# The ring of weight slots moved by 192 bytes in every partition

## What is computed

```python
def swiglu(x, w_gate, w_up, w_down):
    return (jax.nn.silu(x @ w_gate) * (x @ w_up)) @ w_down
...
x = layer_norm(ALPHA * x + 0.5 * swiglu(x, ffn_w_gate[l, 0], ffn_w_up[l, 0], ffn_w_down[l, 0]), ln_g[l, 0], ln_b[l, 0])
x = layer_norm(ALPHA * x + hybrid_mixer(x, w_in[l], ...), ln_g[l, 1], ln_b[l, 1])
x = layer_norm(ALPHA * x + memory_attention(x, mem, xq_w[l], xkv_w[l], xo_w[l]), ln_g[l, 2], ln_b[l, 2])
x = layer_norm(ALPHA * x + 0.5 * swiglu(x, ffn_w_gate[l, 1], ffn_w_up[l, 1], ffn_w_down[l, 1]), ln_g[l, 3], ln_b[l, 3])
```

## Time and profile before

| | us |
|---|---|
| median of 3 runs | 1128.38 (1127.18 to 1129.8) |
| the profiled execution | 1126.32 |
| its span, first to last instruction | 1124.3 |

### The profile page before, as it was taken

One profiled execution on the slowest core, in us unless ns is written; L12 is line 12 of the kernel. 1 busy time (PEld: TensorE's weight loads), 2 busy tenths in 40 slices (PEclk: granted clock), 3 DMA queues, 4 the chain that ended last, 5 costly groups with the idle time before them and its releaser, 6 DMA issues.

```text
span 1124.3 us, 17750 instructions
## 1 busy us (share of the span) xinstructions
PE 1114.1 (99%) x6752; PEld 992.1 (88%) x6752; DVE 776.9 (69%) x1274; ACT 531.9 (47%) x913; POOL 35.5 (3%) x51
## 2 busy tenths in 40 slices
PE   9999999999999999999999999999999999999997
PEld 7899999988888888888898888889899999998886
DVE  4998898753338588774894865557898888863326
ACT  4555555543325477643463453436355555552222
POOL 2000000000002011000000000000000000000000
PEclk9999999999999999999999999999999999999999
DMA  8533333363222222342243242231233333353301
GB/s 286 201 113 113 107 101 111 96 211 94 94 75 89 80 77 84 104 150 75 75 157 126 88 156 75 73 97 58 75 127 99 113 113 96 113 185 99 108 21 75
DMA packets 34121, 123.37 MB, mean 110 GB/s; under 512 B 3916, under 2 KB 3932, under 8 KB 33792
## 3 DMA queue, kind: packets, MB, share of 16 engines
q1 hardware_dynamic: 30528, 109.07, 30.3%
q0 software_dynamic: 3520, 13.29, 3.5%
HBM read 120.23 MB, written 2.11 MB: 109 GB/s over the span
## 4 chain that ended last, share of the span: by engine, by line
PE 94%; DVE 3%; DMA 2%; ACT 1%; issue 0%; DVEq 0%; SPq 0%
PE ps L515 19%; PE ps L516 19%; PE ps L517 19%; PE ps L593 10%; PE ps L594 10%; PE ps L595 10%; DMA raw<-in_units 2%; PE ps L817 1%; PE ps L532 1%; PE ps L796 1%; PE ps L884 1%; PE ps L868 1%; PE ps L789 0%; PE ps L788 0%; PE ps L980 0%
## 5 line engine op out<-in xcount | busy, mean ns | idle before, releaser
L1572 DVE TENSOR_TENSOR wlo<-raw,whi 128x1024 fp32r<-128x1024 f32 x124 | 151.8, 1230 | 171.8 <-ACT whi L1046 170.8
L1046 ACT ACTIVATE whi<-raw 128x1024 fp32r<-128x1024 f32 (+1 forms) x131 | 134.4, 1033 | 135.3 <-PE ps L517 124.2
L515 PE MATMUL ps<-whi,hhi 128*128 128x512 f32 x480 | 187.9, 391 | 0.0
L517 PE MATMUL ps<-whi,hlo 128*128 128x512 f32 x480 | 186.9, 389 | 0.0
L516 PE MATMUL ps<-wlo,hhi 128*128 128x512 f32 x480 | 186.8, 389 | 0.0
L515 PE MATMUL ps<-xth,whi 128*128 128x512 f32 (+1 forms) x340 | 129.6, 381 | 0.0
L517 PE MATMUL ps<-xth,wlo 128*128 128x512 f32 (+1 forms) x340 | 127.5, 375 | 0.0
L516 PE MATMUL ps<-xtl,whi 128*128 128x512 f32 (+1 forms) x340 | 127.4, 375 | 0.0
L517 PEld LDWEIGHTS ps<-whi,hlo 128*128 128x128 f32 x480 | 90.1, 188 | 19.0
L515 PEld LDWEIGHTS ps<-whi,hhi 128*128 128x128 f32 x480 | 90.1, 188 | 18.5 <-ACT km L1046 0.3
L516 PEld LDWEIGHTS ps<-wlo,hhi 128*128 128x128 f32 x480 | 90.2, 188 | 17.9
(11 more groups left out here) (258 smaller groups left out, 2639.1 us busy)
## 6 DMA issues: line engine op xcount, KB each, us to landing
raw<-in_units SPq DMA_DIRECT2D x204, 512.0 KB, 3.5
xraw<-in_units POOLq DMA_DIRECT2D x1, 2048.0 KB, 13.3
xn<-in_x POOLq DMA_DIRECT2D x4, 512.0 KB, 15.2
gb<-in_ln_g POOLq DMA_DIRECT2D x4, 512.0 KB, 3.8
gb<-in_ln_b POOLq DMA_DIRECT2D x4, 512.0 KB, 5.3
wb<-in_bias_by_key POOLq DMA_DIRECT2D x8, 256.0 KB, 3.0
out<-xn SPq DMA_DIRECT2D x8, 256.0 KB, 2.1
gsp<-g_rows POOLq DMA_DIRECT2D x1, 1024.0 KB, 5.1
```

What stands on the lines that cost most here:

```text
L515: mm(dst, lh, rh, start=start, stop=False)
L517: return mm(dst, ll, rh, start=False, stop=stop)
L1046: return nc.scalar.activation(*a, **k)
L1572: v.tensor_tensor(wlo[c % SPL][:, :], raw[c % RAW][:, :], whi[c % SPL][:, :].bitcast(F32), ALU.subtract).then_inc(lo_done, 1)
```

## The change

Before `whi` is laid out, the cursor goes 192 bytes further, and after `wlo` another 320. So `whi` and `wlo`, and with them all names that are placed from `whi_at` and `wlo_at` (`sbh`, `sbl`, `sth`, `stl`), lie 192 bytes further on. `xn` stays; `raw` and all that comes after it move by 512 bytes. `whi` slot 0 is at 33,088 and `gb` at 100,672 then. The instructions of every engine and their order stay as they are; only addresses in them differ.

```diff
@@ -24,6 +24,7 @@
 FAST0 = 4
 HALF = 256
 SMALL = 5
+SKEW = 192
 
 
 def lin(const, per, i):
@@ -137,10 +138,12 @@
             return t
 
         xn = sb("xn", [P, NB, D])
+        cursor[0] += SKEW
         whi_at = cursor[0]
         whi = [sb(f"whi{s}", [P, D], F32R) for s in range(SPL)]
         wlo_at = cursor[0]
         wlo = [sb(f"wlo{s}", [P, D], F32R) for s in range(SPL)]
+        cursor[0] += 512 - SKEW
         raw = [sb(f"raw{s}", [P, D]) for s in range(RAW)]
         ident = sb("ident", [P, P])
         mlg = sb("mlg", [P, MW])
```

## The result

The changed kernel takes **1136.84 us** (1135.48 to 1137.8, four runs) beside 1128.37: a ratio of 1.0074, interval 1.0061 to 1.0086. It is slower, where 31 us less were forecast. The profiled execution took 1135.98 us with a span of 1133.9, 9.6 more than that of before.

The account below looks back on a forecast made before the run. The PE was taken to bound the kernel, its time nearly the number of matmuls times their distance. Gains of 19.6 + 5.0 + 6.4 = 31.0 us off the 1128.38 median gave 1097.4 us, range 1090 to 1112.

Parts of the forecast that it names:

- Term (c): Ring as moving data, 512 columns, 1824 matmuls: 3.5 ns less each, 6.4 us less; bounds 0 and 12.2.
- Term (b): Ring as weights, 512 moving columns, 888 matmuls of the opening: up to 6.7 ns less each, 5.0 us taken.
- Term (a): Ring as weights, 256 moving columns, 2928 matmuls, mostly in fast tiles: 120 to 113.3 ns each, 19.6 us less.
- Rival 3: Place modulo 128 is not the cause; `seh` is quick by region or single use: 1128.4 us; chance 0.10.
- Rival 1: Only the difference of places counts; ring as moving data gains as weights do, 12.2 us: 1091.6 us; chance 0.25.
- Rival 4: Offset ring costs 10 ns more on each of 2712 matmuls at 512 columns: 7.5 us slower, 1135.9; chance 0.05.
- no other engine: ACT and DVE write and read the moved ring in unchanged times: 0 us; only the PE changes.
- sign at `nup`: In a fast tile, DVE's wait for the PE at `nup` halves from 1.0 to 0.5 us.
- Duration as a clock: In the PE's trace, a matmul's duration is its distance to the next plus 163 ns, used as a finer clock.

Follow-up runs that it names:

- matmul-only chains: Kernel with the layer left out: 24 matmuls per pair of operand places, other engines idle; 226.7 to 233.5 ns each at 512 columns, 113.3 to 120.0 at 256.
- eight matmuls ahead of a tile: Changed kernel plus eight matmuls at difference 0, once, ahead of one early fast tile of each FFN: 1138.41 us profiled, 1132.15 to 1133.15 in four others.

## Why the prediction was wrong

- **Term (c), the sign: the step that failed.** 1824 matmuls with the ring as moving data were to gain 3.5 ns each, and lost 6.6: +12.0 us for -6.4, 18.4 of the 40.6 us between the forecast sum and the measured one. The step took the `kmh` rows, 256 columns, for 512 columns. The matmul-only chains show that at 256 columns a difference of 64 pays and that at 512 it costs, in both directions (6.6 ns at +64, 2.2 at -64). The bounds of 0 and 12.2 excluded a loss without a row that did; nothing in the trace of before was this case, as the text said itself, and a range with both signs was due.
- **Term (b), the sign too.** 888 matmuls were to gain 5.0 us by the idea that the loss sits in the weight load and is one for 256 and 512 columns, and cost 2.1, 7.1 of the 40.6. The `wg` rows had spoken against it. They do not fit the law either: slice 4 of `wg` stands at +64 and had 227 ns for both its matmuls, not 233.3, and 234 and 227 in the changed kernel with every remainder as before. It is 100 wide in place of 128; no run explains it.
- **Term (a), the size.** 19.6 us were forecast, and the fast tiles and the rest gave 5.7 + 0.7 - 1.9 = 4.5: 15.1 of the 40.6. The difference is -64 for `sth` and `sbh` as it had been for `seh`, and 113.3 can be had there: with the x side moved by 64 all 84 matmuls of a tile stood at -64 and took it in the second FFN. What failed is that `seh`'s price was taken for a property of the place. It is one of two courses, and what ran before decides between them; before `seh` there were groups at difference 0. With no such group left in the tile, all 84 ran at 117.8, `seh` too. With such a group back in the changed kernel, a tile took 9.60 and not 9.89.
- **Right: the place is the cause.** Moving `gb` alone took the gain from `seh`. Rival 3 falls with it, and with it the rule of the Trainium skill's page "SBUF — State Buffer", section "Who interferes with whom", as the prediction used it: this case's chains of 512 columns, with every other engine idle, have 226.7 to 233.3 ns by the relative place of the two operands alone.
- **Rival 1, half right.** Only the difference counts, and the two roles are mirror images; but that meant a loss at 512 columns in place of the gain that it was priced at.
- **Rival 4, right in direction and, by luck, nearly in price** (1135.9 for 1136.8), by another mechanism. It put 10 ns on 2712 matmuls against a gain of 19.6; in fact 6.6 fell on 1824 and 2.4 on 888 against 4.5. It decides from a mean of 7.2 ns, and that mean was 5.2: the kernel is slower only because the gain stayed out too. Slower had 0.05 in all, though no row of before priced the ring as moving data at 512 columns.
- **Right: no other engine.** ACT 624 and DVE 685 for the odd place, DVE's busy time 776.9 both times. The sign at `nup` was mis-sized, though: where the ring moved by 64 the tile did shorten by 0.48, and DVE's wait there went from 1.0 to 0.75 (9.7 us over 13), not to 0.5. The PE still ended last, so the time followed in full.
- **Duration as a clock.** 163 ns over the distance holds at 113, 120 and 226; at 233.2 it is 394, 161 over. It ranks groups; distances must be read from starts.

## What to carry to other kernels

For fp32r matmuls of 512 columns, lay weights and moving data at the same remainder modulo 256 bytes: the kernel before did, and every other place tried cost 1 to 3% of each matmul here (128 x 128 weights). For 256 columns a difference of 64 pays up to 5.6%, but it has two courses. A group of twelve at difference 0 in each tile, followed by weights at another place, held the better one in nearly every tile of two kernels; in the chains a lead at difference 0 followed by moving data at another place gave the worse one each time. So look at the distances after such an edit, in more than one execution. Before a price is carried over from one shape to another, measure it at that shape, in a chain of matmuls alone if the kernel has none.

## What the runs showed that was not expected

- The distance of two matmuls depends on the relative place of their operands in SBUF, modulo 256 bytes: 226.7, 228.9, about 233 and 233.3 ns at 512 columns for differences of 0, -64, 128 and +64.
- At 256 columns the order turns, 120 at 0 and 113.3 or 117.8 at +-64, and the last two are steady courses of one and the same pair, over 36 tiles of a kernel or for 24 matmuls of a chain.
- Which course is taken goes with what changed last. In the chains, -64 after 0 is quick when the weights' place changed and slow when the moving data's did, 34 times out of 34. The kernels fit this: where every tile or nearly every one is quick (the ring moved by 64, the x side by 192, and the two with `gb` at difference 0), the weights' place changes within each tile and the moving data's doesn't; where all 84 are at -64 nothing changes within a tile, and the changed kernel was slow in both FFNs, the x side moved by 64 in one. The eight matmuls ahead of a tile do not fit. No run was made to test this, none shows how long a lead must be or what in the chip holds the course, and the physical cause of the whole effect stays open.
- One change of a number from 192 to 64 in the same edit is worth 20 us of 1130, with no instruction moved.
